# Which expert pairs fetch and return their tokens through memory, and which by matrix products

## The chip, the cores and the metric

One NeuronCore of a Trainium2 chip runs the whole program; all arithmetic is in 32-bit floats. The metric is device time in microseconds of one execution. The core has a matrix engine (TensorE, PE in the profile), VectorE (DVE), ScalarE (ACT), GpSimd (POOL) and a queue engine that only starts transfers (SyncE, SP). They run their own instruction streams and meet at semaphores.

## The reference, cut to what matters

The model is one step of a two-layer backbone on 384 tokens (128 context and 256 latent) of width 1024. Each layer has a mixer (layer 0: convolution beside attention; layer 1: retention in both directions), which the change leaves alone, and then a mixture of experts:

```
expert_id = g_idx[:, None] * EXPERTS_PER_GROUP + top_i          # 2 of 16 experts per token
combine = jnp.sum(jax.nn.one_hot(expert_id, N_EXPERTS) * top_w[..., None], axis=1)
hidden = jax.nn.silu(jnp.einsum('nd,edf->nef', x, w_gate)) * jnp.einsum('nd,edf->nef', x, w_up)
y = jnp.einsum('nef,efd->nd', hidden * combine[:, :, None], w_down)
x = x + gate_f * y
```

Every expert has three matrices of 2 MB (gate and up 1024x512, down 512x1024). Both layers together read 192 MB of them.

## The kernel before, in words

**Tiles.** Tokens lie in three tiles of 128. The 16 experts are worked in 8 pairs, numbered 0 to 7. A pair takes up to 64 tokens (`CAP`) of either expert as the two halves of one tile of 128 columns. If an expert has more, the pair runs overflow units of 64 more tokens each, in a branch on the count (L786).

**One pair on TensorE (L741 to L806).** The gathered tokens `gT` are multiplied with the gate matrices (`up(0)`), then with the up matrices (`up(1)`); each is 16 products, which the profile shows as 32 instructions. Then the next pair's tokens are brought into place, VectorE makes `hid = silu(gate) * up` (L1717), TensorE turns it (`hid_turn`, L677), ScalarE copies it out (`hidT`, L1162), and `down(0)`, `down(1)` follow (L683).

**How tokens come in.** Pair 0 is gathered by products: `gather` (L692) multiplies the token tiles by a 0/1 matrix of picks, 24 products of 128x128x128. Pairs 1 to 7 are gathered by row number: VectorE makes the picks (L1624), three small products turn them into row numbers (`token_rows`, L654), VectorE copies these (L1641), GpSimd starts an indirect DMA from a copy of the tokens in memory (`hd`, L1341), and TensorE turns the fetched tile with 8 transposes (`turn_tokens`, L664). ScalarE copies either into `gT` (`gathered`, L1100).

**How results go back.** Pairs 0 to 6 are copied by ScalarE (L1172) and stored to `yd` in memory (L1104). When pair 6 is done and its stores have landed, GpSimd starts six indirect DMAs that fetch, for each token tile, the row of its first and of its second expert (L1351). ScalarE scales the first (`scale_back`, L1141), VectorE adds the second, multiplies by the gate row and adds to `x` (`back_to_x`, L1682 to L1684). In pair 7 `back_to_x(0)` stands ahead of `hid` on VectorE. Pair 7's own result is scattered by products: its weighted picks are turned (L698), the result is scaled (`gated`, L1690), six products (L703) spread it over the tokens, and VectorE adds them to `x` (L1696).

**Weights.** SyncE fills eight slots of 2 MB in the order of `STREAM`; slot places come from `MOE_SLOTS`. A fill waits until ScalarE has declared the slot's previous matrix free (`expert_free`, L1153 to L1202). The returned rows land in the slot of pair 6's first down matrix, which no later matrix of the stage uses.

Of the kernel before, what the change touches and what calls it, by code (L numbers as in the profile page):

```python
# [14 lines left out]
P = 128  # L15
# [28 lines left out]
YROWS = (PAIRS - 1 + MORE) * P  # L44
# [50 lines left out]
MOE_SLOTS = ((2, 3, 6, 7, 4, 0, 5, 1), (4, 3, 6, 0, 2, 5, 7, 1))  # L95


def plan_stream():
# [12 lines left out]
    put("moe", 0, range(6 * PAIRS), MOE_SLOTS[0])  # L111
# [5 lines left out]
    for n, (kind, layer, c) in enumerate(seen):  # L117
        put(kind, layer, [c], [(3, 2, 0, 1)[n % 4]])
    put("moe", 1, range(6 * PAIRS), MOE_SLOTS[1])

# [20 lines left out]
BACK = ((0, 0, 3), (1, 0, 4), (0, 1, 7), (2, 0, 0), (1, 1, 1), (2, 1, 2))  # L141
# [8 lines left out]
def unit_counts(l, p):  # L150

    n = (UNITS - 1) * (PAIRS * l + p)
    return 4 * n + (UNITS - 1) * l, 4 * n - (UNITS - 1) * l, 2 * n + 3 * (UNITS - 1) * l, (UNITS - 1) * ((PAIRS - 1) * l + p)
# [10 lines left out]
def backbone_kernel(nc, x_in, cst, par, fgain, cache_k, cache_v, st_in, mod_w, in_w, out_w, w_gate,  # L164
# [3 lines left out]
    with ExitStack() as ctx:  # L168
# [37 lines left out]
        def cutter(*areas):  # L206
# [27 lines left out]
        wl, wl2, there = m(TT, 2), m(TT, 2), m(2, TT)  # L234
# [10 lines left out]
        back = [slot(MOE_SLOTS[l][0]).rearrange("p (a b) -> p a b", a=4) for l in range(2)]  # L245
# [59 lines left out]
            "hidT_mm", "hidT_copied", "down_mm", "y_copied", "pair_stored", "rows_ready", "y1_scaled"))  # L305
        yd_filled, combined, selw_ready, selT_mm, selT_copied, y_gated, scat_mm, x_added = map(sem, (
# [55 lines left out]
        def _(sp):  # L362
# [32 lines left out]
            for i, (kind, l, c) in enumerate(STREAM):  # L395
# [3 lines left out]
                if kind != "moe":  # L399
                    free(i)  # L400
                    if BEFORE[i] == INDEX[("moe", 0, 6 * PAIRS - NSLOT)]:
                        sp.wait_ge(combined, 2)
# [22 lines left out]
        def _(pe):  # L425
# [183 lines left out]
            def experts(l):  # L609
# [40 lines left out]
                def token_rows(p):  # L650

                    pe.wait_ge(sel_ready, base + p + 1)
                    for t in range(TT):
                        mm = pe.matmul(PS[:, 7, p:p + 1], (sel_ov if p == 1 else sel)[:, t, :], C[:, C_TOK + t:C_TOK + t + 1],  # L654
                                       start=t == 0, stop=t == TT - 1)
                    mm.then_inc(idx_mm, 1)

                def turn_tokens(p):

                    pe.wait_ge(g_loaded[p % 2], 16 * ((p + 1) // 2 + (4 if p % 2 else 3) * l))  # L660
                    for half in range(2):
                        for i in range(4):
                            k = 4 * half + i
                            mm = pe.transpose(PS[:, 2 + half, i * P:(i + 1) * P], G[:, p % 2, k * P:(k + 1) * P], ident)  # L664
# [36 lines left out]
                def scatter(n):  # L701
                    t, half, bank = BACK[n]
                    return pe.matmul(PS[:, bank, :], selT[:, t, :], ygate[cnd(t)][:, half * 512:half * 512 + 512],  # L703
                                     start=True, stop=True)
# [15 lines left out]
                def last_overflow(a, b, c, W):  # L720
# [15 lines left out]
                    for n in range(2 * TT):  # L736
                        mm = scatter(n)
# [3 lines left out]
                def pair(p):  # L741
                    g, last = base + p, p == PAIRS - 1
                    a, b, c, _ = unit_counts(l, p)
                    pe.wait_ge(gath_copied, 2 * g + 2)
                    if last:
# [5 lines left out]
                    if not last:  # L751
                        turn_tokens(p + 1)
                    else:
                        pe.wait_ge(selw_ready, l + 1)
                        turn_picks(sel).then_inc(selT_mm, 1)
                    if p == PAIRS - 2:
                        pe.wait_ge(silu_done, g + 1)
                        gate_rows(s, (7, 0, 1, 7), [0])
# [9 lines left out]
                    need(pe, y_copied, 2 * ((PAIRS - 1) * l + p))  # L768
                    need(pe, y_gated, 4 * l)
                    need(pe, ov_act, b)  # L770
                    down(0, W[4:6]).then_inc(down_mm, 1)
                    if p == PAIRS - 2:
# [3 lines left out]
                    if last:  # L776
                        pe.wait_ge(selT_copied, l + 1)
                        for n6 in range(2 * TT):
                            if n6 < 3:
                                pe.wait_ge(y_gated, 4 * l + (1, 2, 3)[n6])  # L780
                            elif n6 == 4:
                                pe.wait_ge(y_gated, 4 * l + 4)
                            scatter(n6).then_inc(scat_mm, 1)
                    step = last_overflow if last else overflow
                    da, db, dc = (5, 3, 5) if last else (4, 4, 2)
                    with pe.If(n > CAP):  # L786

                        if last:
                            pe.wait_ge(x_added, 6 * l + 6)
                        else:  # L790
                            pe.wait_ge(gath_copied, 2 * g + 4)
                            pe.wait_ge(y_copied, 2 * ((PAIRS - 1) * l + p) + 2)
                            if p == PAIRS - 2:
                                pe.wait_ge(gate_copied, 4 * s + 4)
                        step(a, b, c, W)
                        with pe.If(n > 2 * CAP):
                            with pe.Fori(1, UNITS - 1) as u:
                                step(u * da + a, u * db + b, u * dc + c, W)
# [1171 lines left out]
```

## Time and profile before

| | us |
|---|---|
| median of 3 runs | 1478.54 (1473.84 to 1479.14) |
| the profiled execution | 1474.42 |
| its span, first to last instruction | 1472.5 |
| TensorE busy | 1288.9 (88%) |
| VectorE / ScalarE / GpSimd busy | 404.1 / 283.0 / 145.2 |
| expert stage of layer 0, pair 0 to last sum | 344.2 to 671.2 |
| expert stage of layer 1, pair 0 to end | 1214.1 to 1472.5 |

"Busy" is a share over stages with different limits. In the rows, PE is a product and PEld the load of its weights; "x48" merges 48 instructions and the time beside it runs from the first to the end of the last; the bracket holds the idle time ahead of the row and what ended it. "PEq L805" is a branch of TensorE's own instruction stream, "issue" a stop for which the profile shows no cause.

### The profile page before, as it was taken

The page shows a single profiled execution, that of the slowest core. Times are in us where ns is not written, and L with a number is a line of the kernel's source. Part 1 is how long each engine was busy: PE and PEld are TensorE (multiplying, and loading weights), DVE is VectorE, ACT ScalarE, POOL GpSimd, SP SyncE. Part 2 cuts the span into 40 slices and gives each one's busy share as a digit, 9 for nine tenths or more (in the row PEclk, how much of TensorE's full clock was granted, in tenths as well). Part 3 has the DMA queues.
Part 4 walks back from the last instruction along what each step waited for, and adds up shares of the span by engine and source line. Part 5 has one row for each costly group of instructions (what it writes and reads, how often), then busy time and mean ns, then how long its engine had stood idle before and what let it go on. Part 6 is the DMA issues. An engine that isn't in the chain of part 4 may idle for free. (4 is left out here: it accounts for less than half of the span.)

```text
span 1472.5 us, 12662 instructions
## 1 busy us (share of the span) xinstructions
PE 1288.9 (88%) x4937; PEld 620.5 (42%) x4937; DVE 404.1 (27%) x860; ACT 283.0 (19%) x622; POOL 145.2 (10%) x149
## 2 busy tenths in 40 slices
PE   4999799989887878677999989998999889888784
PEld 1543445445333333234445445544554463333231
DVE  0149886042000000414101223202422541000006
ACT  2111243132010110114120221211122231110112
POOL 0079700000000000101000000001000000000001
PEclk9999899989998999799999999999999979998997
DMA  9628899245999984621322321323243528999993
GB/s 398 257 80 337 355 423 414 90 164 231 423 427 428 425 355 191 266 68 62 114 82 97 118 82 65 116 73 118 72 142 116 221 101 344 426 427 425 428 426 157
DMA packets 36672, 351.30 MB, mean 239 GB/s; under 512 B 4065, under 2 KB 9185, under 8 KB 17633
## 3 DMA queue, kind: packets, MB, share of 16 engines
q1 hardware_dynamic: 22608, 315.34, 52.8%
q0 software_dynamic: 6048, 22.02, 3.7%
q10 hardware_dynamic: 7920, 12.59, 2.3%
q8 instruction: 70, 1.15, 0.3%
q14 instruction: 26, 0.21, 0.0%
HBM read 329.75 MB, written 20.19 MB: 238 GB/s over the span
## 5 line engine op out<-in xcount | busy, mean ns | idle before, releaser
L486 PE MATMUL PS<-ring,hT 128*128 128x512 f32 x912 | 396.9, 593 | 0.1
L671 PE MATMUL PS<-ring,hT 128*64 128x512 f32 x864 | 233.3, 622 | 35.2 <-DMA ring<-moe_w_gate 9.5
L486 PEld LDWEIGHTS PS<-ring,hT 128*128 128x128 f32 x912 | 172.1, 190 | 211.4 <-issue 210.6
L671 PEld LDWEIGHTS PS<-ring,hT 128*64 128x64 f32 x864 | 78.9, 143 | 147.0 <-issue 145.3
L683 PE MATMUL PS<-ring,area 128*64 128x512 f32 x448 | 119.3, 619 | 8.1 <-issue 3.9
L671 PE MATMUL PS<-area,hT 128*64 128x512 f32 x288 | 100.2, 635 | 24.8 <-PEq L805 10.1
L1717 DVE TENSOR_TENSOR area<-area,PS 128x512 f32<-128x512 f32 x16 | 11.0, 687 | 325.8 <-PE PS L671 325.7
L826 PE MATMUL PS<-ring,area 128*128 128x512 f32 x192 | 87.8, 616 | 1.4 <-ACT area L1300 1.4
L671 PEld LDWEIGHTS PS<-area,hT 128*64 128x64 f32 x288 | 33.3, 146 | 82.8 <-issue 81.4
L444 PE MATMUL PS<-ring,cond 128*32 128x512 f32 x384 | 51.1, 654 | 18.6 <-DMA ring<-mod_w 18.6
L683 PEld LDWEIGHTS PS<-ring,area 128*64 128x64 f32 x448 | 39.9, 142 | 57.7 <-issue 55.9
L1492 DVE SCALAR_TENSOR_TENSOR area<-area,V 128x414 f32<-128x414 f32 x90 | 63.5, 751 | 0.2
L826 PEld LDWEIGHTS PS<-ring,area 128*128 128x128 f32 x192 | 37.9, 199 | 47.9 <-issue 47.7
L1370 POOL TENSOR_SCALAR area<-area 128x128 f32<-128x128 f32 x32 | 20.0, 640 | 365.8 <-PE PS L890 193.6
L1325 POOL TENSOR_SCALAR area<-area,V 128x414 f32<-128x414 f32 x30 | 49.4, 1648 | 0.0
L1260 ACT ACTIVATE area<-PS 128x512 f32<-128x512 f32 x30 | 17.8, 596 | 161.3 <-PE PS L486 161.3
L1341 POOL DMA_INDIRECT area<-hd,idx x14 | 13.4, 960 | 337.3 <-DVE idx L1641 337.3
L683 PE MATMUL PS<-area 128*64 128x512 f32 x128 | 43.8, 606 | 2.9 <-issue 2.1
L486 PE MATMUL PS<-hT,ring 128*128 128x384 f32 x128 | 44.5, 513 | 1.5 <-DVE hT L1448 1.5
L1100 ACT ACTIVATE hT<-PS 128x512 f32<-128x512 f32 x32 | 17.6, 595 | 140.0 <-PE PS L664 121.3
L1834 DVE TENSOR_TENSOR area<-PS,area 128x384 f32<-128x384 f32 x16 | 8.2, 552 | 130.7 <-PE PS L884 130.7
L591 PE MATMUL PS<-ring 128*128 128x512 f32 x96 | 41.5, 592 | 0.0
(241 smaller groups left out, 1248.9 us busy)
## 6 DMA issues: line engine op xcount, KB each, us to landing
ring<-mod_w SPq DMA_DIRECT2D x24, 2048.0 KB, 14.3
ring<-moe_w_gate SPq DMA_DIRECT2D x24, 2048.0 KB, 22.5
ring<-moe_w_down SPq DMA_DIRECT2D x24, 2048.0 KB, 26.3
ring<-moe_w_up SPq DMA_DIRECT2D x24, 2048.0 KB, 22.2
ring<-in_w SPq DMA_DIRECT2D x21, 2048.0 KB, 8.2
area<-moe_w_up SPq DMA_DIRECT2D x8, 2048.0 KB, 19.8
area<-moe_w_down SPq DMA_DIRECT2D x8, 2048.0 KB, 24.9
area<-moe_w_gate SPq DMA_DIRECT2D x8, 2048.0 KB, 22.9
```

Of the source, the lines that this page charges most:

```text
L444: mm = pe.matmul(PS[32 * j:32 * j + 32, MOD_BANK[l] + g % 3 % 2, :], cond[:, 2 * part + kk, :], wslot(i)[:, kk, j * 512:j * 512 + 512], st ...
L486: mm = pe.matmul(out, lhs(k), rhs(k), start=n == 0, stop=n == KD - 1)
L591: mm = pe.matmul(PS[:, 2 * t + half, :], lhs, wslot(i)[:, k, half * 512:half * 512 + 512], start=n == 0 and k == 0, stop=n == 2 and k == 3)
L671: mm = pe.matmul(PS[64 * e:64 * e + 64, j, :], g[:, k, 64 * e:64 * e + 64], W[e][:, k, :], start=k == 0, stop=k == KD - 1)
L683: mm = pe.matmul(PS[64 * e:64 * e + 64, 5 + half, :], hidT[:, k, 64 * e:64 * e + 64], W[e][:, k, half * 512:half * 512 + 512], start=k == ...
L826: mm = pe.matmul(PS[:, UNTIL[("out", j, part)] % 3, :], mixT[:, k, cols(t)], wslot(i)[:, k, half * 512:half * 512 + 512], start=k == 0, st ...
L1100: act.activation(gT[:, 4 * half:4 * half + 4, :].rearrange("p a b -> p (a b)"), PS[:, 2 + half, :], ACT.Copy).then_inc(gath_copied, 1)
L1260: act.activation(dst[:, b, :], PS[:, bank, :], ACT.Silu if a[0] in "fb" else ACT.Copy, scale=DK ** -0.5 if a[0] == "k" else 1.0).then_inc( ...
L1325: pool.tensor_scalar(ctap[:, j % 2, :], apad[:, 3, j:j + CVN], V[:, w + j:w + j + 1], None, ALU.mult).then_inc(pool_chain, 1)
L1341: pool.indirect_dma_start(G[:, p % 2, :], None, hd[l], bass.IndirectOffsetOnAxis(idx[:, p:p + 1], 0)).then_inc(g_loaded[p % 2], 16)
L1370: w = pool.tensor_scalar(kd[:, i, :], ktok[:, t, o:o + P], dec[:, 1, d * RH + a:d * RH + a + 1], None, ALU.mult)
L1492: i = dve.scalar_tensor_tensor(cv[:, b, :], apad[:, b, j:j + CVN], V[:, o:o + 1], cv[:, b, :], ALU.mult, ALU.add)
```

## The change

`DIRECT = PAIRS - 2 = 6` divides the pairs anew. Pairs 1 to 5 are gathered by products as pair 0 is (pairs "1 to 6", counted from one); pairs 6 and 7 are gathered by row number. Pairs 0 to 5 return through memory; pairs 6 and 7 are scattered by products, each with its own set of PSUM banks. The fetch of the returned rows starts when pair 5 is done; pair 7 works all three tiles off ahead of its `hid`. The rows land in the slot of matrix 34 (pair 5's first down matrix), so that matrices 42 to 47 move on by one slot. The fills of the retention stage use the same four slots in another order, and one wait of theirs for the landing slot is gone.

```diff
+DIRECT = PAIRS - 2
-MOE_SLOTS = ((2, 3, 6, 7, 4, 0, 5, 1), (4, 3, 6, 0, 2, 5, 7, 1))
+MOE_SLOTS = ((2, 3, 6, 7, 4, 0, 5, 1), (4, 3, 6, 1, 0, 5, 7, 2))
+LANDING = 6 * DIRECT - 2
+def moe_slots(order):
+    n = len(order)
+    return [order[(c if c < LANDING + n else c + 1) % n] for c in range(6 * PAIRS)]
...
-        back = [slot(MOE_SLOTS[l][0]).rearrange("p (a b) -> p a b", a=4) for l in range(2)]
+        back = [slot(MOE_SLOTS[l][LANDING % NSLOT]).rearrange("p (a b) -> p a b", a=4) for l in range(2)]
...
# TensorE, pair(p)
-                    if not last:
-                        turn_tokens(p + 1)
-                    else:
-                        pe.wait_ge(selw_ready, l + 1)
+                    if p + 1 < DIRECT:
+                        pe.wait_ge(sel_ready, DIRECT * l + p + 2)
+                        gather(0, sel).then_inc(gath_mm, 1)
+                        gather(1, sel).then_inc(gath_mm, 1)
+                    elif p + 1 < PAIRS:
+                        turn_tokens(p + 1)
+                    if direct:
+                        need(pe, x_added, 6 * d)
+                        pe.wait_ge(selw_ready, d + 1)
                         turn_picks(sel).then_inc(selT_mm, 1)
...
-                    if p < PAIRS - 2:
-                        token_rows(p + 2)
+                    if DIRECT <= p + 3 < PAIRS:
+                        token_rows(p + 3)
+                    if p == DIRECT:
+                        gate_rows(s, (0, 1, 2, 3), [0])
+                        pe.wait_ge(gath_copied, 2 * g + 4)
+                        gate_rows(s, (0, 1, 2, 3), [1])
...
-                    down(0, W[4:6]).then_inc(down_mm, 1)
-                    if p == PAIRS - 2:
-                        pe.wait_ge(gate_copied, 4 * s + 1)
-                        gate_rows(s, (7, 0, 1, 7), [1])
-                    down(1, W[4:6]).then_inc(down_mm, 1)
-                    if last:
-                        pe.wait_ge(selT_copied, l + 1)
+                    for half in range(2):
+                        down(half, W[4:6]).then_inc(down_mm, 1)
+                    if direct:
+                        pe.wait_ge(selT_copied, d + 1)
...
# GpSimd
-                for p in range(1, PAIRS):
+                for p in range(DIRECT, PAIRS):
...
-                pool.wait_ge(expert_free[2], base + PAIRS - 1)
+                pool.wait_ge(expert_free[2], base + DIRECT)
                 for t in range(TT):
+                    if t == 2:
+                        pool.wait_ge(gate_copied, 8 * l + 8)
...
# VectorE, pair(p)
+                    if DIRECT <= p + 3 < PAIRS:
+                        picks(p + 3, sel_ov).then_inc(early_ready, 1)
+                    if p + 1 <= DIRECT:
+                        dve.wait_ge(gath_mm, 2 * g + 2)
+                        if p + 1 < DIRECT:
+                            picks(p + 1, sel).then_inc(sel_ready, 1)
                         else:
-                            dve.wait_ge(gath_mm, 2 * g + 2)
-                        picks(p + 2).then_inc(sel_ready, 1)
...
+                            link(picks(p + 1, sel))
+                            weighted(p + 1, sel).then_inc(selw_ready, 1)
...
                     else:
-                        back_to_x(0)
+                        dve.wait_ge(selT_mm, d)
+                        link(picks(p, sel))
+                        weighted(p, sel).then_inc(selw_ready, 1)
+                        for t in range(TT):
+                            back_to_x(t)
...
+                        dve.wait_ge(gate_copied, 4 * s + 4)
+                        dve.wait_ge(pair_stored, 16 * DIRECT * (l + 1))
```

ScalarE scales all three tiles ahead of pair 7's silu, and copies the gate rows in pair 6 behind `hidT`. The overflow unit of a scattered pair (`last_overflow`, now `direct_overflow`) waits for the pair's own sums first, and then gathers, multiplies, turns its picks, scales, scatters and adds before TensorE goes on. Before, only pair 7 took this form; now pair 6 does too.

## Rows read from the trace of the kernel before

**Rows 1.** The page's slices of 36.8 us: GB/s moved.
```profile
GB/s 398 257 80 337 355 423 414 90 164 231 423 427 428 425 355 191 266 68 62 114 82 97 118 82 65 116 73 118 72 142 116 221 101 344 426 427 425 428 426 157
```
**Rows 2.** Windows, layer 0, pairs 0 to 2: us, busy PE PEld DVE ACT POOL, clock, DMA, GB/s.
```profile
344.19:369.72 25.53, 23.12 (x114) 9.17 (x115) 6.87 (x29) 4.65 (x7) 2.00 (x2) 1.00 0.75 296
369.72:398.19 28.47, 23.73 (x115) 9.28 (x115) 1.41 (x3) 3.37 (x6) 0.95 (x1) 1.00 1.01 425
398.19:424.06 25.87, 23.12 (x115) 10.05 (x115) 1.40 (x3) 3.37 (x6) 0.95 (x1) 1.00 1.01 427
```
**Rows 3.** Windows, layer 1: pairs 0 to 3, and pair 7 to the end.
```profile
1214.12:1239.85 25.73, 23.12 (x115) 9.18 (x115) 6.87 (x29) 4.65 (x7) 1.99 (x2) 1.00 0.75 298
1239.85:1265.62 25.77, 23.11 (x114) 10.04 (x115) 1.40 (x3) 3.37 (x6) 0.94 (x1) 1.00 1.01 425
1265.62:1295.77 30.15, 25.67 (x114) 11.13 (x115) 1.40 (x3) 3.37 (x6) 0.94 (x1) 0.95 1.01 424
1295.77:1323.33 27.56, 24.81 (x114) 10.54 (x115) 1.40 (x3) 3.37 (x6) 0.94 (x1) 0.94 1.01 427
...
1423.00:1472.50 49.50, 30.71 (x115) 11.29 (x115) 22.58 (x26) 10.61 (x17) 5.64 (x6) 0.81 0.55 226
```
**Rows 4.** Timeline of PE, layer 0: pair 2's transposes, pair 3's start after the branch.
```profile
412.07 1.09 PE L664 MATMUL PS<-C,area 128*128 128x128 f32 x8
...
424.06 7.09 PE L671 MATMUL PS<-area,hT 128*64 128x512 f32 x32 [2.42 <-PEq L805]
```
**Rows 5.** Timeline of PE: three up products that waited for their matrices.
```profile
528.44 8.59 PE L671 MATMUL PS<-ring,hT 128*64 128x512 f32 x32 [4.16 <-DMA ring<-moe_w_up]
...
1334.60 0.61 PE L671 MATMUL PS<-area,hT 128*64 128x512 f32 x1 [2.49 <-DMA ring<-moe_w_up]
...
1399.58 0.61 PE L671 MATMUL PS<-area,hT 128*64 128x512 f32 x1 [2.48 <-DMA ring<-moe_w_up]
```
**Rows 6.** Timeline of PE: pair 6 of layer 0 and its overflow; layer 1's first gather.
```profile
537.89 1.88 PE L478 MATMUL PS<-area,C 128*128 128x512 f32 x4
...
550.97 5.60 PE L692 MATMUL PS<-area 128*128 128x128 f32 x48 [0.74 <-issue]
...
582.39 7.09 PE L671 MATMUL PS<-area,hT 128*64 128x512 f32 x32 [0.67 <-PEq L801]
...
1205.18 8.26 PE L692 MATMUL PS<-area 128*128 128x128 f32 x48 [1.80 <-DVE area L1624]
```
**Rows 7.** Timeline of PE: pair 7 of layer 0, then of layer 1.
```profile
609.85 1.11 PE L677 MATMUL PS<-C,area 128*128 128x128 f32 x4 [13.04 <-DVE area L1717]
611.81 9.57 PE L683 MATMUL PS<-ring,area 128*64 128x512 f32 x32 [0.84 <-issue]
...
628.26 5.60 PE L692 MATMUL PS<-area 128*128 128x128 f32 x48 [1.53 <-DVE area L1634]
...
1448.38 1.12 PE L677 MATMUL PS<-C,area 128*128 128x128 f32 x4 [9.58 <-DVE area L1717]
...
1458.71 1.13 PE L703 MATMUL PS<-area,hT 128*128 128x512 f32 x2
...
1461.39 2.74 PE L703 MATMUL PS<-hT 128*128 128x512 f32 x6
```
**Rows 8.** Timeline of DVE, layer 0: first returned rows, and the overflow's sums.
```profile
605.28 1.28 DVE L1682 SCALAR_TENSOR_TENSOR ring<-ring,area 128x1024 f32<-128x1024 f32 x1 [32.04 <-DMA ring<-yd,idx]
...
667.51 3.67 DVE L1696 TENSOR_TENSOR x<-x,PS 128x512 f32<-128x512 f32 x6 [5.51 <-PE PS L703]
```
**Rows 9.** Timeline of SP, layer 0: the two gate matrices of pair 2 are issued.
```profile
369.52 0.80 SPq L364 DMA_DIRECT2D ring<-moe_w_gate  x2
```
**Rows 10.** Timeline of PE, layer 1: a stop inside pair 2's gate product.
```profile
1271.87 4.88 PE L671 MATMUL PS<-ring,hT 128*64 128x512 f32 x21 [1.92 <-issue]
```
**Rows 11.** The page's DMA issues: KB each, median us from issue to landing.
```profile
yd<-area ACTq DMA_DIRECT2D x14, 512.0 KB, 11.0
ring<-yd,idx POOLq DMA_INDIRECT x8, 8.5
```

More of the change, by code:

```diff
@@ L110, in plan_stream @@
         put(kind, layer, [c], [n % 5])
-    put("moe", 0, range(6 * PAIRS), MOE_SLOTS[0])
+    put("moe", 0, range(6 * PAIRS), moe_slots(MOE_SLOTS[0]))
     seen = []
@@ L117, in plan_stream @@
     for n, (kind, layer, c) in enumerate(seen):
-        put(kind, layer, [c], [(3, 2, 0, 1)[n % 4]])
-    put("moe", 1, range(6 * PAIRS), MOE_SLOTS[1])
+        put(kind, layer, [c], [(3, 0, 1, 2)[n % 4]])
+    put("moe", 1, range(6 * PAIRS), moe_slots(MOE_SLOTS[1]))
 plan_stream()
@@ L699, in turn_picks, with scatter @@
                     return mm
[L701 to L704, printed above, removed]
+                def scatter(p, n):
+                    t, half = BACK[n]
+                    return pe.matmul(PS[:, BACK_BANK[p - DIRECT][n], :], selT[:, t, :],
+                                     ygate[cnd(t)][:, half * 512:half * 512 + 512], start=True, stop=True)
                 def overflow(a, b, c, W):
@@ L736, in last_overflow @@
                     for n in range(2 * TT):
-                        mm = scatter(n)
+                        mm = scatter(p, n)
                     mm.then_inc(ov_pe, 1)
@@ L797, in pair @@
                             with pe.Fori(1, UNITS - 1) as u:
-                                step(u * da + a, u * db + b, u * dc + c, W)
+                                if direct:
+                                    direct_overflow(p, u * da + a, u * db + b, u * dc + c, W)
+                                else:
+                                    overflow(u * da + a, u * db + b, u * dc + c, W)
                         with pe.Else():
@@ L1155, in pair @@
                         act.sem_inc(expert_free[1], 1)
-                    if not last:
+                    if p + 1 < PAIRS:
                         gathered(p + 1)
-                    else:
-                        act.wait_ge(selT_mm, l + 1)
+                    if direct:
+                        act.wait_ge(selT_mm, d + 1)
                         act.activation(selT.rearrange("p a b -> p (a b)"), PS[:, 7, 0:NT], ACT.Copy).then_inc(selT_copied, 1)
@@ L1179, in pair @@
                         store(ysb, at, pair_stored)
-                    db = 3 if last else 4
+                    db = 3 if direct else 4
                     with act.If(n > CAP):
-                        if last:
-                            last_overflow(a, n)
+                        if direct:
+                            direct_overflow(a, n)
                         else:
@@ L1196, in pair @@
                             act.sem_inc(ov_act, db * (UNITS - 2))
-                            if not last:
+                            if not direct:
                                 act.wait_ge(ov_stored, 16 * (o + 1))
@@ L1204, in pair @@
                         act.sem_inc(ov_act, db * (UNITS - 1))
-                        if not last:
+                        if not direct:
                             need(act, ov_stored, 16 * o)
@@ L1764, in pair @@
                                 more_picks(p).then_inc(ov_dve, 1)
-                                unit(u * (5 if last else 4) + a, u * (3 if last else 4) + b, u * dc + c)
+                                unit(u * da + a, u * db + b, u * dc + c)
                         with dve.Else():
@@ L1785, in pair @@
                         dve.sem_inc(ov_key, UNITS - 2)
+                    if direct and not last:
+                        dve.wait_ge(x_added, 6 * d + 6)
                     dve.nop()
```

184 lines of the change are left out of this document (85 added, 99 removed).

## The prediction, made before the change was run

> **What bounds the kernel now.** I numbered the pairs 0 to 7 as the code does; "pair 6" is the seventh. First the page's slices: during both expert stages (slices 10 to 14 and 34 to 38) the core moves 423 to 428 GB/s, the most of the whole run, so the weight stream is full there [rows 1]. Second, each pair as a window of its own: the early pairs take 25.53 to 28.47 us, and a pair without any extra stop takes 25.8 us [rows 2, 3]. Third, where TensorE waits for weights. In layer 0 it does so last at 528.44, the up matrices of pair 6; in layer 1 the same pair resumes at 1399.58 [rows 5]. Between 1334.60 and 1399.58 twelve matrices came in, so a step of two costs the queue 10.83 us, 32.5 us a pair. TensorE needs 25.8. So the stage begins with TensorE setting the pace, eats up its lead, and ends with the queue setting it. Fourth, the end of each stage. Pair 6 of layer 0 overflows (more than 64 tokens for an expert), and so does pair 7: a second gather of 48 instructions stands in each [rows 6, 7]. In pair 7 TensorE then waits 13.04 us for `hid` in layer 0 and 9.58 us in layer 1 [rows 7], because VectorE, which makes `hid`, is held by rows that come back from memory (32.04 us idle, released by that DMA) [rows 8]. After that wait the down product takes 9.57 instead of 7.09 us.
>
> **The gather of pairs 1 to 5.** Removed per pair: 8 transposes, 1.09 us. Added: 24 products, shown as 48 instructions, 5.60 us in the overflow of pair 6 [rows 4, 6]. Both stand between up and hid_turn (before: 412.07, right behind the up product), so ScalarE's copies and the wait for `hidT` follow as before, and the price is 5.60 - 1.09 = 4.5 us a pair. The three small products for row numbers go too, but they lay in the time of the hidT copy and give nothing. Bounds: 3.8 us, if they did count for their 0.73, to 7.2, the difference with the first gather of layer 1 at the lower clock (8.26 us, with one wait in it, [rows 6]). I take 4.5, since the warm row is the same operation in the same stage. Five pairs: 22.5 us a layer, on TensorE.
>
> **What hides it.** I carry TensorE's own chain forward. Layer 0: pair 0 starts at 344.19 as before; windows of 25.53, 28.47, 25.87, then three of 25.8, and 22.5 for the gathers: pair 6 starts at 524.0 and its up product ends 13.9 later, at 537.9. Before it ended at 528.44 + 8.59 = 537.0. So 0.9 us of 22.5 are left; the rest goes into waits for weights and their cold stretches. Layer 1: windows of 25.73 (from 1214.12), 25.77, 30.15, 27.56, twice 25.8, plus 22.5: pair 6 starts at 1397.4, up ends at 1411.3; before, 1399.58 + 7.0 = 1406.6. Left: 4.7 us.
> Is the queue early enough? One gathered tile and one stored tile of 0.52 MB ride with each pair's 12.58 MB; without the first, at 427 GB/s, a step of two falls from 10.83 to 10.42 us. Against that slots come free later: the fourth pair of fills was issued at 369.52, when pair 0 was finished [rows 9], and will be 4.5 later, so the queue runs dry for some 2.4 us there and for about 2 at two later pair ends. With them, and a landing 3.7 us behind the stream (that fits 528.44 and 1399.58 alike), the up matrices of pair 6 land at 527 and 1399, and are wanted at 530.9 and 1404.3. TensorE stays ahead by 4 and 5 us of slack: it is now the bound throughout.
>
> **Extra stops.** The seven windows in which nothing waited for weights hold 8.9 us over 25.8 (2.7, 4.4, 1.8): an "issue" stop of 1.92 us inside a product, with slow instructions after it [rows 3, 10]. These were carried above. Pairs 3 to 5 of layer 0 and 4 and 5 of layer 1 may have had such stops under their waits for weights and would show them now: 5 x 1.27 = 6 us; below nothing is excluded, above it is 5 x 4.4 = 22. I take 5, 2.5 a layer.
>
> **Pair 6.** Up end to down end takes 0.9 (transposes) + 0.5 (turned picks) + 0.5 (hid_turn) + 3.8 (both gate rows, 1.88 each, [rows 6]) + 7.1 = 12.8 us, where the split order took 13.2 (537.0 to 550.2): -0.5. Then six scatter products, 5.4 us from 1458.71 on [rows 7], as pair 7 has them. Without overflow (layer 1) the next pair starts 0.2 + 5.4 + 2.4 (the branch, 2.42 in [rows 4]) behind the down product, not 3.2, and pair 7 starts at 1411.3 + 12.8 + 0.2 + 5.4 + 2.4 = 1432.1, 9.1 later than 1423.00. With overflow (layer 0) the second gather waits for the sums: 6.9 us from down end to gather as in pair 7 (621.38 to 628.26, [rows 7]), not 0.74: +6.2. The overflow unit itself took 31.4 us (550.97 to 582.39); the direct form of pair 7 took 628.26 to 671.2, 42.9 us [rows 7, 8], and 0.9 to go on: +12.4. Pair 7 starts at 582.4 + 0.9 - 0.5 + 6.2 + 12.4 = 601.4, 19 later. That wait holds everything on TensorE, for nothing else is queued there; the next pair's matrices load meanwhile.
> Edits at nothing: VectorE makes the picks of the next pair and two more weighted picks (0.56 us each) where it sat idle more than 20 us a pair; if that cover went, a gather would start up to 1.1 later. Its new wait for pair 5's store stands ahead of the scaling of pair 6's result only: stored at about 1396.5, landed 11.0 later [rows 11] at 1407.5, wanted at 1421; the sums of pair 6 behind it are what would be late. They run beside the scatter, as in pair 7. ScalarE scales the returned rows ahead of pair 7's silu: 3.5 us from 1428 on, silu is due at 1439.
>
> **Pair 7.** The returned rows are now asked for at the end of pair 5's store (11.0 us) and land 8.5 us after issue [rows 11]: about 1428 in layer 1, long before in layer 0. VectorE works them off (three times 3.75 us, three operations like the row at 605.28, 1.28) from 1432.5 to 1444, and `hid` is due at 1446: hidden, with 2 us to spare. So hid_turn comes 13.9 + 1.0 = 14.9 us after the start of the pair: 616.3 in layer 0 (before 609.85), 1447.0 in layer 1 (before 1448.38). Down is warm and ends 7.1 after it starts: 617.6 + 7.0 = 624.6 against 621.3, +3.3; and 1448.3 + 7.1 = 1455.4 against 1458.7, where the scatter began, -3.3. The remainder of both stages is the same code. The sharing of slots costs nothing: the last matrix (pair 6's down slot) is issued at 1425, lands at 1446 with the returned rows' 3.1 MB in the stream, and is wanted at 1448.
>
> **Sum.** 3.3 - 3.3 + 5 = +5 us. On the profiled execution, 1474.42 (span 1472.5 and 1.9 around it), 1479.4. The median of the runs is 1478.54, 4.1 above that execution, with runs from 1473.84 to 1479.14; I put the forecast between, at **1481**.
>
> **Rules weighed.** Row: 1.92 us of "issue" inside straight code and 2.2 to 3.2 after each pair's branch. The Trainium skill (Runtime: NRT & Kernel Launch, Instruction fetch mechanics) says that fetching is sequential and mostly hidden, and that a taken branch to a page not yet held stalls. By that rule the 340 added instructions are free, the straight-code stop is not explained, and the sum would be 1476 to 1479; the trace disagrees with it once and agrees at each branch. Row: after the 13.04 us wait the down product ran 9.57 us [rows 7], and the last window, which holds the like wait, has a granted clock of 0.81 [rows 3]; the parts that ran without one stand at 1.00, the upper level. The Trainium skill (TensorE: Matmul & The Clock Gate, HAM oscillation) says that waits for DMA throw the engine back to the half clock; this is the third rival's mechanism, and it speaks for the change.
>
> **The rivals.**
> A, slower: TensorE is alone on the path and the gathers double its instruction stream between the products; stops of the kind of [rows 10] come in most pairs. For it: the row's 4.4 us, in a window with a full stream; against it: five of seven free windows have little or none. It decides from two stops a layer more than I count; at four in all, 4 x 4.4 less the 5 counted, +12.6: 1493. With two, 1485.
> B, faster: TensorE, never starved, stays at full clock and the stops do not recur. For it: the windows at 1.00 are those without waits [rows 2, 3]. Against it: two of the slow windows (0.95, 0.94) had no wait for weights. Then neither the 8.9 nor the 5 are there: +5 - 13.9 = -8.9 us, 1472 beside the forecast's 1481.
> C, the queue stays the bound: free slots come so late that pair 6's weights miss by some 4 us and cost a cold stretch of 2.5 in each layer. For it: slack of 4 and 5 us only; against it: less traffic. +13: 1494.
> D, the change does not do what it says: the rows return late after all and pair 7 still waits in layer 1. Landing was 8.5 us outside and would be longer in a full stream; 5 us more cost 3: 1484.
>
> **How the numbers follow.** Forecast 0.48 (with D, 0.05 of it), A 0.27, B 0.20, C 0.05. Its own range is 1475 to 1487. 0.5%, about 7.4 us, is what a measurement here can tell from no change: below 1471.1 is faster, above 1485.9 slower. B reaches that in most of its weight with 0.17; A and C give 0.27 and the forecast's upper edge 0.04: slower 0.31; within 0.52. The range that holds 8 in 10 cuts the ends of B and A: 1469 to 1493.
>
> **What would show it.** Gather products of about 5.6 us behind each up product; no wait for weights after pair 1 in either layer, and a granted clock of 1.00 in those windows; pair 6 starting at 524 to 527 and 1397 to 1400; pair 7 at about 602 to 604 and 1433 to 1435; no wait of TensorE for `hid` in pair 7, so its down product at 7.1 us. Wrong would be: waits for weights in pair 5 or 6 (C), more "issue" stops (A), windows of 30.3 us flat (B), or a wait before hid_turn in pair 7 (D).

## The result, and the profile after

The changed kernel takes **1488.48 us** (median of 7 runs, 1482.82 to 1492.28) against 1478.54 (7 runs). The ratio is 1.0066, with a 95% interval of 1.0038 to 1.0095. The forecast was 1481, within 0.5% of no change; the time lies inside the range of 1469 to 1493, but it is a small loss and not "no change", and it lies above the forecast's own range of 1475 to 1487. A slower kernel (above 1485.9) had been given a chance of 0.31. The profiled executions lie 17.0 us apart, not 9.9: that of the changed kernel took 1491.44 us (span 1489.5), 3.0 above its median, and that of before lay 4.1 below its own.

First the stretch in which only gathers were added. Windows of the kernel after, pairs 0 to 5 of layer 0 and then of layer 1, columns as in [rows 2]:

```profile
344.48:374.50 30.02, 27.04 (x149) 13.04 (x149) 1.25 (x2) 4.76 (x7) 0.00 (x0) 1.00 0.68 281
374.50:405.91 31.41, 28.73 (x148) 14.40 (x149) 1.25 (x2) 3.47 (x6) 0.00 (x0) 0.95 1.01 415
...
497.61:524.69 27.08, 24.25 (x109) 9.84 (x109) 1.92 (x2) 3.37 (x6) 0.00 (x0) 0.94 1.01 426
...
1350.02:1381.64 31.62, 29.29 (x154) 15.07 (x155) 1.97 (x4) 3.47 (x6) 0.97 (x1) 0.95 1.01 426
sum 360.48, PE 328.35 PEld 162.02 DVE 20.10 ACT 44.02 POOL 4.01; mean PE 27.36 PEld 13.50 DVE 1.68 ACT 3.67 POOL 0.33
```

A pair with a gather takes 29.6 to 31.6 us; the base of the forecast was 25.8 + 4.5 = 30.3, and 25.8 for pair 5. The sum, over all twelve windows, is 360.48; the base gives 354.6. So all extra stops and slow stretches together are 5.9 us. The granted clock is 1.00 in only six of the twelve windows; the forecast had it in all. The six at 0.94 or 0.95 each begin with a stop of 1.97 to 2.37 us, the others with 0.69 to 1.84 (though a stop of 2.86 us ahead of pair 7 of layer 1, shown below, brought no slow product).

What TensorE waited for, before (the first fence) and after (the second); columns: total us, times, longest:

```profile
PE PS L677 <- DVE area L1717: 22.8, 3, 13.0
PE PS L671 <- DMA ring<-moe_w_up: 14.0, 6, 4.2
PE PS L671 <- DMA ring<-moe_w_gate: 13.5, 4, 4.9
```
```profile
PE PS L679 <- PEq L818: 24.5, 12, 2.9
PE PS L679 <- PEq L814: 10.9, 1, 10.9
PE PS L685 <- DVE area L1733: 6.0, 2, 5.5
```

The waits for expert weights are gone and the wait for `hid` has shrunk from 22.8 to 6.0 us. New is one stop of 10.9 us, put down to TensorE's own instruction stream (PEq); L814 is the way out of the overflow branch, L818 that of a pair without overflow. Timeline of PE after, layer 0, from pair 6's second gather through its overflow to pair 7's scatter:

```profile
557.76 5.60 PE L700 MATMUL PS<-area 128*128 128x128 f32 x48 [1.53 <-DVE area L1645]
...
594.25 2.74 PE L711 MATMUL PS<-hT 128*128 128x512 f32 x6
607.87 1.09 PE L679 MATMUL PS<-area,hT 128*64 128x512 f32 x1 [10.89 <-PEq L814]
...
625.68 0.66 PE L685 MATMUL PS<-C,area 128*128 128x128 f32 x4 [0.40 <-DVE area L1733]
...
634.19 1.12 PE L711 MATMUL PS<-area,hT 128*128 128x512 f32 x2
```

VectorE's sums, for which TensorE waits there by the code, take up only the first part of that stop (timeline of DVE, same stretch):

```profile
597.02 3.68 DVE L1705 TENSOR_TENSOR x<-x,PS 128x512 f32<-128x512 f32 x6 [5.51 <-PE PS L711]
```

They end at 600.70. The other 7.2 us are the way out of the overflow branch (experiments 1 and 3). After the stop the first products take 1.06 instead of 0.59 us until 613.87, and the pair's gate and up products 16.86 instead of 13.9 (+2.9). Pair 7's scatter is 12.9 us later than before (634.19 against 621.31).

Layer 1: pair 7 on PE, then the fetches of the third tile's rows on POOL and their first use on ACT and DVE:

```profile
1444.89 7.48 PE L679 MATMUL PS<-ring,hT 128*64 128x512 f32 x33 [2.86 <-PEq L818]
...
1464.87 1.12 PE L685 MATMUL PS<-C,area 128*128 128x128 f32 x4 [5.55 <-DVE area L1733]
1466.83 8.96 PE L691 MATMUL PS<-ring,area 128*64 128x512 f32 x32 [0.84 <-issue]
1475.72 1.13 PE L711 MATMUL PS<-area,hT 128*128 128x512 f32 x2
```
```profile
1430.57 0.94 POOL L1362 DMA_INDIRECT area<-yd,idx  x1 [5.77 <-ACT gate_row L994]
1431.81 0.94 POOL L1362 DMA_INDIRECT area<-yd,idx  x1 [0.30 <-issue]
```
```profile
1457.21 1.15 ACT L1153 ACTIVATE area<-area 128x1024 f32<-128x1024 f32 x1 [11.21 <-DMA area<-yd,idx]
```
```profile
1460.30 1.28 DVE L1691 SCALAR_TENSOR_TENSOR area<-area 128x1024 f32<-128x1024 f32 x1 [5.30 <-DMA area<-yd,idx]
```

The last fetch was issued at 1431.81 and its rows were there at 1460.30, 28.5 us later. ScalarE waited for the third tile's rows until 1457.21, 26.6 after their issue at 1430.57, with its silu queued behind. VectorE works that tile off before `hid`, so TensorE waits 5.55 us, and its down product runs 8.96 instead of 7.09 us. (The third tile's two fetches had been held 5.77 us by the wait for the gate rows; experiment 8 says why that cost nothing.) Layer 1 starts 14.4 later than before; its scatter comes 17.0 later (1475.72 against 1458.71), so the stage added 2.6.

### The profile page after: what moved, and what is told of

Its sections match the earlier page's. It is cut to its first block and busy times, and to the rows that moved or that the text cites. A ratio compares the mean times of both kernels' runs of the same rounds, so it can differ in the third digit from the quotient of the medians.

```text
span 1489.5 us, 13411 instructions
## 1 busy us (share of the span) xinstructions
PE 1335.9 (90%) x5322; PEld 664.3 (45%) x5322; DVE 426.1 (29%) x887; ACT 281.7 (19%) x619; POOL 136.7 (9%) x139
## 5 line engine op out<-in xcount | busy, mean ns | idle before, releaser
L679 PE MATMUL PS<-ring,hT 128*64 128x512 f32 x896 | 244.1, 618 | 21.3 <-PEq L818 16.6
L679 PEld LDWEIGHTS PS<-ring,hT 128*64 128x64 f32 x896 | 84.6, 142 | 129.1 <-issue 126.0
L679 PE MATMUL PS<-area,hT 128*64 128x512 f32 x256 | 100.2, 635 | 19.9 <-PEq L814 10.9
L700 PE MATMUL PS<-area 128*128 128x128 f32 x672 | 83.4, 287 | 5.6 <-DVE area L1645 3.1
L700 PEld LDWEIGHTS PS<-area 128*128 128x128 f32 x672 | 80.9, 202 | 15.5 <-issue 13.2
L679 PEld LDWEIGHTS PS<-area,hT 128*64 128x64 f32 x256 | 31.6, 145 | 77.9 <-issue 76.5
L1112 ACT ACTIVATE hT<-PS 128x512 f32<-128x512 f32 x32 | 18.7, 597 | 165.2 <-PE PS L700 137.8
```

The source lines that it names most:

```text
L679: mm = pe.matmul(PS[64 * e:64 * e + 64, j, :], g[:, k, 64 * e:64 * e + 64], W[e][:, k, :], start=k == 0, stop=k == KD - 1)
L700: mm = pe.matmul(PS[:, 2 + half, i * P:(i + 1) * P], h[:, t, k * P:(k + 1) * P], pick[:, t, :], start=t == 0, stop=t == TT - 1)
L1112: act.activation(gT[:, 4 * half:4 * half + 4, :].rearrange("p a b -> p (a b)"), PS[:, 2 + half, :], ACT.Copy).then_inc(gath_copied, 1)
```

## Experiments

What I held after the result: the loss is two waits that the return part makes, one at the branch in layer 0 and one for late rows in layer 1. All diffs are against the changed kernel.

**1. The wait behind the branch.**

```
-                    pe.wait_ge(ov_dve, c + 5)          # end of direct_overflow
+                    if hold:                           # hold = p != DIRECT
+                        pe.wait_ge(ov_dve, c + 5)
...
                     if direct:
                         need(pe, x_added, 6 * d)
+                        if p > DIRECT:
+                            pe.wait_ge(ov_dve, c)
                         pe.wait_ge(selw_ready, d + 1)
                         turn_picks(sel).then_inc(selT_mm, 1)
```

> The changed kernel, with TensorE's wait for the sums of pair 6's overflow moved from the end of the overflow unit (ahead of the branch) to pair 7, ahead of its turned picks. In the changed kernel layer 0 stops 10.89 us between the overflow's scatter and pair 7, 3.7 of it while VectorE adds, 7.2 after it. Theory F (the branch jumps over the unused loop, its code has to be fetched, and the wait keeps the fetch from starting until the sums are done): the fetch now runs beside the scatter, the stop falls to 1 to 3 us, the slow start of the gate product behind it (2.9 us) goes too; in all 9 to 12 us less than the changed kernel, so a ratio to before of 0.998 to 1.001 instead of 1.0066. Rival G (the stop has a fixed part that does not care where the wait is): only the 3.7 us of the sums are saved, the stop is 7 us, ratio 1.004.

Ratio to before 1.0024 (0.9999 to 1.0049), median 1479.70 of 10 runs. Timeline of PE, layer 0, and DVE's sums, which no longer hold TensorE:

```profile
594.29 2.74 PE L711 MATMUL PS<-hT 128*128 128x512 f32 x6
597.69 0.61 PE L679 MATMUL PS<-area,hT 128*64 128x512 f32 x1 [0.66 <-PEq L819]
...
615.13 0.65 PE L685 MATMUL PS<-C,area 128*128 128x128 f32 x4 [3.01 <-DVE area L1738]
625.34 1.13 PE L711 MATMUL PS<-area,hT 128*128 128x512 f32 x2
```
```profile
597.07 3.68 DVE L1710 TENSOR_TENSOR x<-x,PS 128x512 f32<-128x512 f32 x6 [6.97 <-PE PS L711]
```

The stop falls from 10.89 to 0.66 us and the products start at the higher clock (0.61 us each). The sums end at 600.75 here too: TensorE now stands still neither for them nor for the 7.2 us behind them. From the overflow's last scatter product to pair 7's scatter it is 28.3 us instead of 37.2. Part of the gain comes back: `hid` is now 3.01 us late, since VectorE's chain (sums, picks, three returned tiles) has not moved while TensorE has; in layer 1 `hid` is 6.13 us late. So the ratio lies above the 0.998 to 1.001 that I expected.

**2. All returned rows behind `hid`.**

```
                     if p == PAIRS - 1:          # VectorE; on ScalarE scale_back likewise
-                        for t in range(TT):
-                            back_to_x(t)
                     ... hid ...
+                    if last:
+                        for t in range(TT):
+                            back_to_x(t)
```

> The changed kernel with the returned rows of pair 7 worked off behind hid and not ahead of it: ScalarE makes the silu and copies hidT before it scales, VectorE makes hid before back_to_x of all three tiles. Theory (in layer 1 the rows of the third tile land at 1457 to 1460, some 15 us later than I had forecast, and silu and hid queue behind them): TensorE's wait for hid in layer 1 falls from 5.55 to 0.4 us and the down product from 8.96 to 7.1, 7 us less than the changed kernel, ratio to before 1.002; layer 0 is as it was (the rows were there long before). Rival (the third tile's work, done by 1464, is only moved in front of the scaling of pair 7's result and is paid there): 0 to 3 us less, a new wait of the scatter products for VectorE.

Ratio 1.0120 (1.0084 to 1.0155), median 1493.66 of 4 runs: no gain at all. It may be worse than the change itself, but the intervals overlap (1.0038 to 1.0095 there) and the profiled spans, 1490.9 and 1489.5 us, are close. My theory was wrong: what its rival named, a new wait of the scatter, came. Timeline of PE, layer 0 and layer 1:

```profile
618.60 0.66 PE L685 MATMUL PS<-C,area 128*128 128x128 f32 x4 [0.38 <-DVE area L1731]
633.31 2.05 PE L711 MATMUL PS<-area,hT 128*128 128x512 f32 x2 [6.12 <-DVE area L1699]
...
1475.26 2.04 PE L711 MATMUL PS<-area,hT 128*128 128x512 f32 x2 [6.13 <-DVE area L1699]
```

The wait for `hid` is 0.38 in both layers, but VectorE now has 11.5 us of returned tiles in front of the scaling (L1699) that the scatter needs, and the down product covers only 7.1. The scatter waits 6.1 us and starts slowly (2.05 us for two products that take 1.12 elsewhere), in layer 0 too, where the old order had no wait.

**3. Transfers kept out of the branch's way.** In layer 0 the next matrices are asked for only when pair 6's sums are done.

```
+                    if l == 0 and c == 46:
+                        sp.wait_ge(ov_dve, unit_counts(0, PAIRS - 1)[2])
                     fill(i, expert(l, c))
```

> The changed kernel; in layer 0 the queue engine waits, before it issues pair 7's two down matrices and all that follows, until VectorE has done pair 6's overflow sums. So the transfer engines are empty at the stop between pair 6 and pair 7, where in the changed kernel they run full until about 610. Theory F' (the code behind the branch comes through the same transfer engines and waits behind the weights): the 7.2 us between the last sum and pair 7's first product fall to 3 to 4 us, as at the end of pair 7 of layer 0 in the kernel before (3.8 us, engines empty). Rival (the jump costs the same whatever the traffic): 7 us. The held matrices are issued at 601, land by 613 and are wanted at about 627: no wait for them by either.

One run: 1483.83 us. Timeline of PE, layer 0:

```profile
589.59 2.74 PE L713 MATMUL PS<-hT 128*128 128x512 f32 x6
600.18 1.08 PE L681 MATMUL PS<-area,hT 128*64 128x512 f32 x1 [7.86 <-PEq L816]
```

The stop is 7.86 instead of 10.89; without the 3.7 for the sums that is 4.2 us instead of 7.2. In the changed kernel the transfers ran at 430 to 434 GB/s from 597 to 607.87; here they stood still from about 590 on, until the held fills, issued at 596.17, came in at 597. So 3 of the 7.2 us go with the traffic.

The traces also show what TensorE waited for. The DMA view lists a queue of the kind "instruction"; its packets carry program code (73 of them, 1.20 MB in the whole run, so 16 KB each). In windows of 0.1 us one such packet shows up at 604.6 to 604.7 us in the changed kernel, at 597.0 to 597.1 here and at 594.2 to 594.3 in experiment 1 (columns: packets, MB, share of the 16 engines in the window):

```profile
q8 instruction: 1, 0.02, 66.3%
```
```profile
q8 instruction: 1, 0.02, 65.3%
```
```profile
q8 instruction: 1, 0.02, 62.4%
```

The same place in all traces in which pair 6 is scattered and overflows, in us (experiments 5, 7 and 8 stand below):

| | TensorE free to go on | code packet | first product |
|---|---|---|---|
| changed kernel | 600.70 (sums done) | 604.6 to 605.7 | 607.87 |
| experiment 2 | 595.75 (sums done) | 599.3 to 600.4 | 602.46 |
| experiment 7 | 594.00 (sums done) | 598.0 to 599.0 | 601.23 |
| experiment 8 | 603.40 (sums done) | 607.6 to 608.7 | 610.75 |
| experiment 3 | 596.03 (sums done) | 597.1 to 598.1 | 600.18 |
| experiment 1 | 597.03 (scatter done) | 594.2 to 595.2 | 597.69 |
| experiment 5 | 591.06 (scatter done) | 589.4 to 590.4 | 592.53 |

Where the wait stands ahead of the way out, the packet sets out only after the sums: 3.6 to 4.2 us after them in a full stream, 1.1 us with the stream stopped. Where it does not, the packet comes while the scatter still runs. In all but experiment 1, where the scatter ended later, the first product follows 2.0 to 2.2 us after the packet has landed. So what the full stream costs here is 3 us of waiting ahead of the packet. The view does not name the engine whose code a packet carries; that it is TensorE's is read from these steady 2 us.

**4. The gather part alone.** Pairs 1 to 5 gathered by products; pair 6 still stored and returned through memory, as before.

```
-DIRECT = PAIRS - 2
+ROWS = PAIRS - 2
+DIRECT = PAIRS - 1
...        # gather and pick conditions go by ROWS, scatter and return by DIRECT
```

> Only the gather part of the change: pairs 1 to 5 gathered by products, 6 and 7 by row number; pairs 0 to 6 return through memory and only pair 7 is scattered, in the order of the kernel before (one back_to_x ahead of hid, two behind it). If the gathers cost TensorE what is left of 4.5 us a pair once the waits for weights are used up, pair 6's up product ends 1 to 2 us later in layer 0 and 3 to 4 in layer 1, the waits of 13 and 9.6 us in pair 7 stay, and the kernel takes 4 to 6 us more than before, ratio 1.003 to 1.004. Then the other half of the change's 10 us is in its return part. Rival: the gathers carry the whole loss, ratio 1.006 to 1.008, and the return part is even. Second rival: they cost nothing, ratio 1.000, and the return part carries it all.

Ratio 0.9985 (0.9961 to 1.0008), median 1473.46 of 10 runs: this is the case in which the gathers cost nothing and the return part carries the whole loss. Timeline of PE, layer 0's pair 6 up end and both waits for `hid`:

```profile
537.03 1.09 PE L676 MATMUL PS<-C,area 128*128 128x128 f32 x8
...
608.04 1.11 PE L689 MATMUL PS<-C,area 128*128 128x128 f32 x4 [12.26 <-DVE area L1735]
...
1444.67 1.12 PE L689 MATMUL PS<-C,area 128*128 128x128 f32 x4 [10.03 <-DVE area L1735]
```

Pair 6's up product ends where it did before (537.0) in layer 0. In layer 1 it ends 2.2 us later, counted from the start of the layer (194.6 against 192.5 us; expected 3 to 4), and by pair 7's scatter nothing of that is left (243.9 against 244.6). Against the changed kernel (1.0066) the return part carries 0.8%, 12 us.

**5. Both repairs, two tiles ahead and one behind.** Experiment 1, and of the three returned tiles only two ahead of `hid` (and of silu), the third behind:

```
-                        for t in range(TT):     # scale_back on ScalarE, back_to_x on VectorE
+                        for t in range(2):
...
                     ... hid, hidT copied ...
+                    if last:
+                        back_to_x(2)            # on ScalarE scale_back(2)
```

> The changed kernel with TensorE's wait moved as in defer_wait, and in pair 7 only two tiles of returned rows ahead of silu and hid, the third behind them (3.75 us of VectorE beside the down product's 7.1). Theory (the third tile's rows land last, at 1460 in the changed kernel, and are all that holds hid; three tiles behind hid were too many, because 11.2 us do not fit beside a down product): against defer_wait's profile (1479.5) the waits for hid of 3.0 and 6.1 us fall to 0.4 each, both down products run at 7.1 instead of 8.8, no new wait of the scatter: 9 to 11 us less, 1469 for the profile, ratio to before 0.995 to 0.997. Rival (rows of the second tile come late as well, or the work on the third is paid at the scatter): ratio 1.000 to 1.002.

**Ratio 0.9947 (0.9928 to 0.9965)**, median 1467.97 of 8 runs: faster than the kernel before and than the changed one, and the lowest of all forms, though experiment 6 lies within its interval. Timeline of PE, pair 7 of layer 0 and of layer 1:

```profile
592.53 0.61 PE L679 MATMUL PS<-area,hT 128*64 128x512 f32 x1 [1.47 <-PEq L819]
...
607.36 0.66 PE L685 MATMUL PS<-C,area 128*128 128x128 f32 x4 [0.40 <-DVE area L1740]
608.85 7.09 PE L691 MATMUL PS<-ring,area 128*64 128x512 f32 x32 [0.84 <-issue]
...
1440.79 0.66 PE L685 MATMUL PS<-C,area 128*128 128x128 f32 x4 [0.40 <-DVE area L1740]
1442.29 7.09 PE L691 MATMUL PS<-ring,area 128*64 128x512 f32 x32 [0.84 <-issue]
```

Pair 7 up to its scatter, as windows of the changed kernel and then of this one:

```profile
607.87:634.19 26.32, 25.08 (x103) 8.97 (x103) 8.25 (x9) 1.69 (x3) 0.00 (x0) 0.89 0.09 35
1444.89:1475.72 30.83, 24.44 (x104) 9.35 (x104) 12.77 (x12) 3.83 (x5) 0.00 (x0) 0.89 0.41 169
```
```profile
592.53:615.87 23.34, 22.10 (x103) 8.76 (x104) 16.45 (x18) 2.72 (x4) 0.00 (x0) 1.00 0.51 217
1425.96:1449.31 23.35, 22.11 (x104) 8.77 (x104) 13.06 (x12) 3.65 (x5) 0.00 (x0) 1.00 0.54 223
```

The same pair takes 23.3 us in both layers at a granted clock of 1.00, instead of 26.3 and 30.8 at 0.89. With the stop (10.9 down to 1.5) the rows account for 9.4 + 3.0 + 7.5 = 19.9 us; the ratios of 1.0066 and 0.9947 differ by 17.6. So these three places account for the loss to about 2 us. The two profiled executions lie further apart (1491.44 and 1464.94, 26.5 us), since one is 3.0 above its median and the other 3.0 below.

Against the gather part alone (0.9985, and 0.9955 in experiment 6) the repaired return part gives 0.1 to 0.4%, with intervals that overlap: no run here shows that scattering pair 6 gains anything.

**6. The gather part alone, with `hid` ahead of all returned tiles.** The edit of experiment 2, on experiment 4.

> gather_only with hid ahead of all three back_to_x in pair 7, and the silu and the copy of hidT ahead of all scaling. There the rows come back late anyway (VectorE starts on them at about 604 and 1440) and VectorE is the bound from then on. Theory: hid and the down product drop out of that chain, but the 11.2 us of back_to_x and the four scalings stay in it: about 4 us less in layer 0 and 2 to 3 in layer 1, ratio to before 0.994 against gather_only's 0.9985. Rival: as in hid_first, what hid gains the scatter waits, ratio 0.998 to 1.000.

Ratio 0.9955 (0.9938 to 0.9972), median 1469.78 of 10 runs. `hid` is on time, but the scatter waits 10.99 us in layer 0 and 8.70 in layer 1 for VectorE (L1705). In the profiled execution it starts at 618.23 and 1452.97, against 618.94 and 1455.39 in experiment 4, whose whole span is only 0.1 us longer (1469.2 against 1469.1); the ratios lie 0.3% apart with intervals that overlap. How much the order alone gives here stays open; its wait has mostly moved, not gone.

**7. A third of the gather products** in pairs 1 to 5.

```
-                        gather(0, sel).then_inc(gath_mm, 1)      # gather(1, sel) likewise
+                        gather(0, sel, 1).then_inc(gath_mm, 1)   # one token tile of three
```

> The changed kernel with the gathers of pairs 1 to 5 reduced from 24 products to 8 (only the first token tile is gathered, so the other two thirds of those pairs' tokens are left out; all else has its full size). It takes 3.7 us a pair off TensorE, 37 in all. Theory (the queue stands only 4 to 5 us behind TensorE in the changed kernel): TensorE runs into waits for weights again, the up product of pair 6 ends only 3 us earlier in layer 0 and 2 to 5 in layer 1, and the kernel is 5 to 9 us faster than the changed one (1491.4 in its profile, so about 1484). Rival (TensorE alone is the bound and the queue far ahead): 30 us or more.

One run: 1500.12 us, and that total says nothing: with other tokens one more pair of layer 1 overflows (a gather of 48 instructions at 1360.56). Layer 0 can be read. Timeline of PE there:

```profile
491.45 8.79 PE L679 MATMUL PS<-ring,hT 128*64 128x512 f32 x32 [2.20 <-DMA ring<-moe_w_up]
...
523.17 7.09 PE L679 MATMUL PS<-ring,hT 128*64 128x512 f32 x32 [2.48 <-DMA ring<-moe_w_up]
530.18 1.09 PE L672 MATMUL PS<-C,area 128*128 128x128 f32 x8
```

18.7 us of products were taken out (5 times 2/3 of 5.6). Pair 6's up product ends 8.4 earlier (530.18 against 538.57), 6.7 when its layer's earlier start (342.75 against 344.48) is taken off, and the waits for weights are back. That is more than the 3 I expected, but the other 12.0 us of the 18.7 only fill what would be waiting: the queue stands close behind TensorE. Against the kernel before, which waited for weights too, the up product ends 5.3 earlier from the start of the layer (187.4 against 192.8 us). So the stream itself runs ahead of before's. That fits the fetched tiles it no longer carries: 0.52 MB in each of five pairs are 6.1 us at 427 GB/s, by my estimate.

**8. Fills held until the rows are in,** layer 1.

```
+                    if l == 1 and c == 46:
+                        for t in range(TT):
+                            sp.wait_ge(y1_back[t], 32)
+                            sp.wait_ge(y2_back[t], 32)
                     fill(i, expert(l, c))
```

> The changed kernel; in layer 1 the queue engine does not issue pair 7's two down matrices before all six fetches of returned rows have landed. Theory (the fetches were issued at 1420 to 1432 and took up to 28 us because the transfer engines were full of weights, where outside the stream they take 8.5): with 4.2 MB less ahead of them the third tile's rows land at about 1445 to 1450 on the changed kernel's clock, TensorE's wait for hid in layer 1 falls from 5.55 to 1 or less. The down matrices land at 1460 and may cost 0 to 3 us there. Rival (the fetch is slow by itself): landing and wait as they were, and the down product later on top.

One run: 1484.84 us. The held matrices are issued at 1449.39. Timeline of ACT and PE, layer 1:

```profile
1448.12 1.15 ACT L1157 ACTIVATE area<-area 128x1024 f32<-128x1024 f32 x1 [3.53 <-DMA area<-yd,idx]
```
```profile
1459.84 0.66 PE L689 MATMUL PS<-C,area 128*128 128x128 f32 x4 [0.40 <-DVE area L1737]
1462.09 7.09 PE L695 MATMUL PS<-ring,area 128*64 128x512 f32 x32 [1.60 <-DMA ring<-moe_w_down]
```

The third tile's rows, issued at 1429.51, are there at 1448.12 (18.6 us, not 26.6), the last ones by 1449.39 (18.6, not 28.5). The wait for `hid` is gone and the down product takes 7.09 us, though its matrix now comes 1.6 us late. So the rows were late because the last fills stood beside them; even so they took more than twice the 8.5 us of [rows 11].

How the two share the transfer engines is in the DMA view, where q0 is the queue of the indirect fetches (packets, MB, share of the engines). Changed kernel, 1424 to 1450; then the kernel before, layer 1, 1438 to 1446:

```profile
q1 hardware_dynamic: 595, 8.70, 79.0%
q0 software_dynamic: 592, 2.17, 20.8%
```
```profile
q0 software_dynamic: 688, 2.50, 77.6%
```

Beside the weights the rows got 2.17 MB in 26 us, 83 GB/s; before, with the weights nearly in (0.44 MB beside the rows), 2.50 MB in 8 us, 313 GB/s. In this experiment it is 87 GB/s until 1440, since the two up matrices still run, and 206 from there to 1448. At such a rate the third tile's fetches, issued 5.77 us late, still stand behind the 2.1 MB of the first two tiles, of which the last rows were in use only at 1451.19.

## Why the prediction was right, and where it was wrong

**Gather, right.** 5.62 us behind each up product, 29.6 to 31.6 us a pair, no wait for weights. Pair 6 of layer 0 started at 524.69 (forecast 524 to 527); that of layer 1 at 1394.4 on before's scale (1408.79 less the shift of 14.4), earlier than the 1397 to 1400 forecast. The gathers hide in queue time: at pair 6's up end 1.3 us of 22.5 are left in layer 0 and 3.4 in layer 1, counted from the start of the layer (forecast 0.9 and 4.7). In the time of the whole kernel experiment 4 finds no cost. The granted clock of 1.00 came in half of the windows only.

**Extra stops, too dear.** 5.9 us against 8.9 carried and 5 added: 8 us fewer. Rival A is out, and the half of rival B that said "the stops do not recur" is partly true. Why they are fewer no run tested. The trace of before has one more clue: its two "issue" stops inside a gate product, 1.92 us up to 1271.87 [rows 10] and 2.47 up to 375.81, each hold a code packet that lands 1.3 to 1.4 us before the product goes on. The changed kernel has no stop inside a product in its twelve windows.

**Pair 6, right up to the last sum.** Second gather at 557.76 (forecast 557.7), sums done at 600.70 (forecast 601.4 - 0.9 = 600.5). **The step that failed is the next one, "and 0.9 to go on".** I gave no row for that 0.9; it is near the 0.67 us of [rows 6], where the branch runs beside products already queued. In the direct form the wait for the sums stands ahead of the jump, so nothing covers it: 7.2 us, then a gate and up product that start at the lower clock (granted 0.50 of full speed from 600.70 to 607.87), 2.9. `hid_turn` came at 625.68, not 616.3. Experiment 1 shows the cause (0.66 when the wait stands behind the branch), experiment 3 that 3 of the 7.2 us are transfer traffic, and the table there that they lie ahead of a packet of code. The forecast had named that wait as one that "holds everything on TensorE", and then did not ask what came after it. The trace of before already held such an exit, behind pair 7's overflow in layer 0. Timeline of PE:

```profile
674.96 3.56 PE L470 MATMUL PS<-C,area 128*128 128x128 f32 x16 [7.49 <-PEq L801]
```

The sums of [rows 8] end at 671.18, 3.8 us before, with the transfers nearly at rest from 668 on (part of the 3.8 may be VectorE's next step, which ended at 674.3). So a price well above 0.9 was there to be read. The Trainium skill (Runtime: NRT & Kernel Launch, Instruction fetch mechanics) says that a taken branch to a page not held has to fetch it by DMA before the engine can go on. The traces agree: the stop is at the branch, and a packet of code lands 2.0 to 2.2 us ahead of the first product. What fills those 2 us, and what holds the packet back in a full stream, no run shows.

**Rows "landing 8.5 us after issue", the second that failed.** 8.5 was a median over eight of before's twelve fetches (9.0 in layer 1), which ran when the weights were nearly in. Here they took up to 28.5, at 83 GB/s beside the weights. "Hidden, with 2 us to spare" thus became a wait of 5.15 us more than planned and 2.45 behind it, most of that the down product at 8.96 (scatter +2.6 instead of -3.3, with pair 7 1.6 earlier than forecast). That is rival D, which I had named and priced at 3 us for 5 us of lateness; the lateness was 20. Experiment 8 and the DMA view show the cause. I had D at 0.05; it came true in layer 1, and is worth 7.5 us of experiment 5's gain.

**Sum.** Forecast +5; in the profiles +17.0. Layer 0: +9.6 over the forecast's scatter. Layer 1: +5.9. Of the 5 that stood apart for more stops nothing is left: -5. Between the layers and in pair 7's own overflow: 17.0 - 12.9 - 2.6 = +1.5. 5 + 9.6 + 5.9 - 5 + 1.5 = 17.0. By medians +9.9. That the time fell inside the range is in part luck: the stops saved 8 us of what these two steps cost.

## What to carry to other kernels

Here a branch was cheap only while products issued ahead of it still ran: move a wait that ends a branch to the first instruction behind it that needs the data, and price a branch behind a wait by itself. When a stop is put down to an engine's own sequencer, look for the code packets in the DMA view. Price an indirect fetch by the stream it will meet, not by its median over the kernel. Test the parts of a change by themselves: here the gather part alone was as fast as before, and nothing shows that the return part gains. When work is moved ahead of or behind the instruction on the path, count how much of it each cover holds (here two tiles ahead of `hid`, one under the down product): all on either side costs a wait.

## What the runs showed of the hardware

- The way out of a branch behind a wait: 6.7 to 7.4 us in a full stream (four traces), 4.2 with fills held back, 0.66 and 1.47 where it could run beside products.
- In it a 16 KB packet of code, taking 1.0 to 1.1 us, sets out 3.6 to 4.2 us after the wait in a full stream and 1.1 us after it without; TensorE's first product came 2.0 to 2.2 us after it had landed.
- Indirect fetches of one tile's rows: up to 28.5 us beside the weight stream, 18.6 with the last fills held, against a median of 8.5 in the kernel before. Their queue moved 83 GB/s beside the weights, 313 with the weights nearly in.
- After the stops of 7.9 to 11.1 us at the branch TensorE's products took 1.06 instead of 0.59 us for 2.6 to 6.0 us, which cost 1.3 to 2.9 us; after 5.6 us of waiting the down product took 8.96 instead of 7.09.
